# Splits of the last six feed-forward tiles ahead of the down projections: one slot of the border plan in place of two

## The chip, the core and the metric

The kernel runs on one core of a Trainium2 chip. The time is the device time of one execution in microseconds. A core has TensorE (PE, matrix products into PSUM), ScalarE (ACT), VectorE (DVE), GpSimd (POOL) and SyncE (SP, which issues the DMAs here). Each runs its own instructions strictly in the order written, and they meet only at semaphores.

## The reference

One inference step of a two-layer hybrid decoder: 512 prompt tokens and 8 sequences of 8 sample tokens go through the same weights, 576 tokens in all, with a model width of 1024. Each layer has a SwiGLU half-step, a recurrent mixer and a second SwiGLU half-step. Cut to the part that the change touches:

```python
D_MODEL, D_FF = 1024, 2816

def _swiglu(h, w_gate, w_up, w_down):
    return (jax.nn.silu(h @ w_gate) * (h @ w_up)) @ w_down

def _trunk(x, c, states, w):
    for l in range(2):
        f1 = _swiglu(adaln_1(x), w_gate[l, 0], w_up[l, 0], w_down[l, 0])
        x = x + 0.5 * (1.0 + gate1) * f1
        x = x + (1.0 + gate2) * mixer_l(adaln_2(x))
        f2 = _swiglu(adaln_3(x), w_gate[l, 1], w_up[l, 1], w_down[l, 1])
        x = x + 0.5 * (1.0 + gate3) * f2
```

All values are fp32. There are four SwiGLU blocks.

## The kernel before, in words

**Products in three parts.** Every fp32 operand of a matmul is split into a high part (rounded to fp32r) and a low part (the rest). ACT writes the high part (`split_high`, L171), DVE subtracts it from the raw value for the low part (`split_low`, L175), and PE multiplies low by high, high by low and high by high (L1489, L1491, L1493). Weights are split as well as activations. All splits show up in the profile under the two helper lines, so they are told apart by their tiles and widths: a weight piece has 1024, 768 or 512 columns, a hidden tile has 576.

**Stages and pieces.** `dense_chain` builds a chain of stages: `up` (gate and up projections, 22 output tiles of 128), `down` (8 output tiles), projections into and out of the mixers. The program has three such chains with the mixers between them; four `up` stages are each followed by their `down` stage. The work of a stage is cut into pieces, each one weight block in SBUF. The pieces of all stages of a chain are numbered through, and PE goes through them in order, saying `piece_done` after each. In a down stage each output tile has three pieces, with 8, 8 and 6 of the 22 hidden tiles (`DOWN_PIECES`). The hidden tiles come in the order 0 to 6, 8 to 21, 7 (`DOWN_ORDER`).

**Buffers.** Raw weights land in three slots (`RAW`), split weights stand in three places (`SPLIT`). A raw slot is free once its low split is done; then SP issues the next load. A split place is free once PE has ended the piece that stood in it, so the high split of piece i + 3 waits for `piece_done` of piece i.

**Hidden tiles.** Tiles 1 to 7 (`IN_TIME`) are split as they are made. Tile 0 and tiles 8 to 21 (`LATE`) are kept raw in `big_buf` and split later: `hidden_high` (L1609) writes the high part to `low_r` on ACT and says `late_high`, `hidden_low` (L1831) writes the low part to `big_r` on DVE and says `late_low`. At the first output tile of the down stage PE waits before each late tile for its `late_low`.

**The order on ACT and DVE** is one loop over the pieces i in each engine's program, cut here to what runs at a border:

```python
for i in range(total + 1):            # ACT; DVE has low(...) and hidden_low(...) in the same places
    ...
    if i + AHEAD < total:             # AHEAD is 2
        high(i + AHEAD)
    ...
    if i in late_at:
        for kt in late_at[i][1]:
            hidden_high(late_at[i][0], kt)
```

`late_tiles_at` (L1195) is the plan of the late tiles, with `end` for the last piece of the up stage: tile 0 and tiles 8 and 9 in the up stage's last unit, tiles 10 to 12 at `end`, 13 to 15 at `end + 1`, 16 to 18 at `end + 2` and 19 to 21 at `end + 3`. `end + 1` is the first piece of the down stage. So at `end + 2` each engine splits the weights of piece `end + 4` and tiles 16 to 18, and at `end + 3` the weights of piece `end + 5` and tiles 19 to 21. The high splits of tiles 18 to 21 also wait for a piece of the up stage's last unit; in the down stages that have one, the modulation of the next sublayer is computed between the pieces (L123, its weights issued by SP at L116).

Of the kernel before, what the change touches and what calls it, by code (L numbers as in the profile page):

```python
# [1014 lines left out]
def dense_chain(k, stages, begin=False, final=False, early=None, constants=None, stored=None):  # L1015
# [23 lines left out]
    with nc.cleanup_on_exit():  # L1039
# [155 lines left out]
        def late_tiles_at():  # L1195

            plan = {}
            for stage in ups:
                q, end = stage.units[-1].pieces[0][0], stage.last
                for i, tiles in ((q + 1, (0,)), (q + 2, (8, 9)), (end, (10, 11, 12)), (end + 1, (13, 14, 15)),  # L1200
                                 (end + 2, (16, 17, 18)), (end + 3, (19, 20, 21))):
                    plan[i] = (stage, tiles)
            return plan
        late_at = late_tiles_at()
        shift_at, mix_at, high_at, low_at = ({} for _ in range(4))
        for number, stage in enumerate(stages):
# [3117 lines left out]
```

How the kernel before makes its waits and increments, by code:

```python
    def load(self, sp, step):  # L112
        slots = len(self.slot)
        if step >= slots:
            sp.wait_ge(self.done, step - slots + 1)
        sp.dma_start(self.slot[step % slots], self.source[step]).then_inc(self.landed[step % slots], 16)
# [1 line left out]
    def products(self, pe, step):  # L118
        k, slots, width = self.k, len(self.slot), self.per * P
        kt, part, slot = step // self.parts, step % self.parts, step % slots
        pe.wait_ge(self.landed[slot], (step // slots + 1) * 16)
        for j in range(4):
            last = pe.matmul(k.psum[self.banks[part]][32 * j:32 * j + NC_WIDE, 0:width],
                             k.cs[:, kt * NC_WIDE:(kt + 1) * NC_WIDE],
                             self.slot[slot][:, j * width:(j + 1) * width], start=kt == 0, stop=kt == KT - 1)
        last.then_inc(self.done, 1)
# [1 line left out]
    def copy(self, act):  # L128
        act.wait_ge(self.done, self.steps)
        width = self.per * P
        if self.parts == 2:
            act.activation(self.by_vector.rearrange("p (a n) -> p a n", a=2), two_halves(self.k.psum_pair(3), width), ACT.Copy)\
                .then_inc(self.copied, 1)
        else:
            act.activation(self.by_vector, self.k.psum[self.banks[0]][:, 0:width], ACT.Copy).then_inc(self.copied, 1)
# [1 line left out]
    def turn(self, pe):  # L137
        pe.wait_ge(self.copied, 1)
        for part, bank in enumerate(self.banks):
            for b in range(self.per):
                at = (part * self.per + b) * P
```

## Time and profile before

| | us |
|---|---|
| median of three runs | 2674.79 |
| lowest and highest of them | 2669.65, 2676.82 |
| the profiled execution | 2666.39 |
| its span | 2664.7 |

| engine | busy, us | share of the span |
|---|---|---|
| PE, matmuls | 2564.0 | 96% |
| DVE | 1604.7 | 60% |
| ACT | 1056.2 | 40% |
| POOL | 646.3 | 24% |

The granted clock of PE was 0.97 of full speed over the whole execution. To read the profile: the page gives totals and groups of instructions, the waits say which engine stood still for which other one, and the timeline lists one engine's instructions in order of time, with the idle time ahead of an instruction and what ended it in brackets. Matmul records overlap, since they are pipelined: the pace is the distance of their starts, not their length.

### The profile page before, as it was taken

Reading aid. Unit: us, or ns where it says so; the run is one execution under the profiler, and the core shown is the slowest. Engines: PE = TensorE matmul, PEld = TensorE weight load, DVE = VectorE, ACT = ScalarE, POOL = GpSimd, SP = SyncE. Lnnn points to the kernel's source line nnn. Section 1 sums busy time; section 2 is a strip of 40 time slices with the busy share of each in tenths; the row PEclk is TensorE's granted clock in tenths of the full one; section 3 lists DMA queues with packets and bytes.
Section 4 is the critical chain, followed back from the end, with each engine's and each line's share of the span. In section 5 each row is a group of like instructions: output and inputs, shape, how many; then the busy total and the mean of one; then the engine's idle time right before and its main releaser. Section 6 shows DMA issues by size and latency. Waiting matters only on the chain. (4 is left out here: it accounts for less than half of the span.)

```text
span 2664.7 us, 52727 instructions
## 1 busy us (share of the span) xinstructions
PE 2564.0 (96%) x22860; PEld 2410.2 (90%) x22860; DVE 1604.7 (60%) x2302; ACT 1056.2 (40%) x1532; POOL 646.3 (24%) x494
## 2 busy tenths in 40 slices
PE   6999999999999899999999999999999989999998
PEld 4999999887787787999999999999989779999997
DVE  5678626665465555677842677852743256777825
ACT  4444414554344322444432544432432334444513
POOL 0455201000010031255501055500100212355301
PEclk8999999999999979999999999999999789999999
DMA  6332455631100014122255322255751113222324
GB/s 237 105 122 94 154 188 189 244 128 52 34 3 3 9 60 163 64 96 95 94 188 177 120 90 96 96 176 181 233 201 60 50 46 111 71 94 92 99 83 133
DMA packets 80144, 301.60 MB, mean 113 GB/s; under 512 B 8985, under 2 KB 14633, under 8 KB 78633
## 3 DMA queue, kind: packets, MB, share of 16 engines
q1 hardware_dynamic: 79912, 298.23, 33.4%
q8 instruction: 181, 2.97, 0.5%
q14 instruction: 51, 0.41, 0.0%
HBM read 287.45 MB, written 10.74 MB: 112 GB/s over the span
## 5 line engine op out<-in xcount | busy, mean ns | idle before, releaser
L175 DVE TENSOR_TENSOR weights_r<-work,weights_r 128x1024 fp32r<-128x1024 f32 (+2 forms) x309 | 389.6, 1261 | 342.8 <-ACT weights_r L171 342.7
L171 ACT ACTIVATE weights_r<-work 128x1024 fp32r<-128x1024 f32 (+2 forms) x309 | 299.6, 970 | 539.4 <-PE banks L1493 304.0
L1374 POOL TENSOR_TENSOR rows<-rows,consts 128x288 f32<-128x288 f32 (+3 forms) x64 | 82.0, 1282 | 720.0 <-ACT consts L1636 720.0
L1491 PE MATMUL banks<-low_r,weights_r 128*128 128x288 f32 (+1 forms) x1064 | 254.8, 298 | 0.0
L1392 PE MATMUL banks<-big_r,weights_r 128*128 128x288 f32 x768 | 227.0, 296 | 0.0
L1393 PE MATMUL banks<-h_r,weights_r 128*128 128x288 f32 x768 | 226.6, 295 | 0.0
L1391 PE MATMUL banks<-h_r,weights_r 128*128 128x288 f32 x768 | 226.5, 295 | 0.0
L1489 PE MATMUL banks<-h_r,weights_r 128*128 128x288 f32 (+1 forms) x808 | 200.9, 306 | 4.7 <-DVE big_r L437 4.7
L1491 PE MATMUL banks<-big_r,weights_r 128*128 128x288 f32 (+2 forms) x800 | 201.9, 298 | 0.0
L175 DVE TENSOR_TENSOR ring_r<-consts,ring_r 128x1024 fp32r<-128x1024 f32 (+1 forms) x87 | 106.1, 1219 | 155.6 <-ACT ring_r L171 155.6
L1489 PE MATMUL banks<-low_r,weights_r 128*128 128x288 f32 (+2 forms) x720 | 182.5, 303 | 16.9 <-DVE low_r L175 12.0
L1493 PE MATMUL banks<-h_r,weights_r 128*128 128x288 f32 (+1 forms) x808 | 195.0, 299 | 0.0
L1491 PEld LDWEIGHTS banks<-low_r,weights_r 128*128 128x128 f32 x1064 | 181.1, 190 | 0.1
L1493 PE MATMUL banks<-low_r,weights_r 128*128 128x288 f32 (+2 forms) x720 | 179.2, 298 | 0.0
L1391 PE MATMUL banks<-low_r,weights_r 128*128 128x288 f32 x576 | 170.1, 295 | 0.0
L1392 PE MATMUL banks<-low_r,weights_r 128*128 128x288 f32 x576 | 169.9, 295 | 0.0
L1393 PE MATMUL banks<-low_r,weights_r 128*128 128x288 f32 x576 | 169.4, 294 | 0.0
L1489 PEld LDWEIGHTS banks<-h_r,weights_r 128*128 128x128 f32 x808 | 137.5, 190 | 24.2 <-issue 8.9
L171 ACT ACTIVATE ring_r<-consts 128x1024 fp32r<-128x1024 f32 (+1 forms) x87 | 89.8, 1032 | 173.1 <-PE banks L1493 155.4
L1489 PEld LDWEIGHTS banks<-low_r,weights_r 128*128 128x128 f32 x720 | 124.8, 191 | 28.7 <-DVE weights_r L175 13.0
L1393 PEld LDWEIGHTS banks<-h_r,weights_r 128*128 128x128 f32 x768 | 144.8, 189 | 0.0
L1391 PEld LDWEIGHTS banks<-h_r,weights_r 128*128 128x128 f32 x768 | 144.3, 188 | 0.4 <-issue 0.4
(584 smaller groups left out, 7134.4 us busy)
## 6 DMA issues: line engine op xcount, KB each, us to landing
work<-w_ff_dram SPq DMA_DIRECT2D x117, 512.0 KB, 3.4
h<-w_mod_dram SPq DMA_DIRECT2D x48, 768.0 KB, 5.1
consts<-w_ff_dram SPq DMA_DIRECT2D x59, 512.0 KB, 3.4
work<-w_down_dram SPq DMA_DIRECT2D x55, 512.0 KB, 3.6
big_buf<-w_mod_dram SPq DMA_DIRECT2D x24, 768.0 KB, 5.8
consts<-w_down_dram SPq DMA_DIRECT2D x33, 512.0 KB, 3.6
work<-w_down_dram SPq DMA_DIRECT2D x33, 384.0 KB, 3.3
work<-w_mod_first_dram SPq DMA_DIRECT2D x24, 512.0 KB, 12.2
```

The lines of the kernel that those rows point to most:

```text
L171: return act.activation(high, raw, ACT.Copy)
L175: return engine.tensor_tensor(low, raw, high.bitcast(F32), ALU.subtract)
L1374: pool.tensor_tensor(k.rows[:, c], k.rows[:, c], k.square[:, c], ALU.add).then_inc(added, 1)
L1391: pe.matmul(out, low[:, w], x_high, start=j == 0, stop=False)
L1392: pe.matmul(out, high[:, w], x_low, start=False, stop=False)
L1393: last = pe.matmul(out, high[:, w], x_high, start=False, stop=j == KT // 2 - 1)
L1489: pe.matmul(out[a], low[:, w], x[a][0], start=begins, stop=False)
L1491: pe.matmul(out[a], high[:, w], x[a][1], start=False, stop=False)
L1493: last = pe.matmul(out[a], high[:, w], x[a][0], start=False, stop=closes)
```

## The change

Tiles 19, 20 and 21 move from the slot `end + 3` to the slot `end + 2`, behind tiles 16, 17 and 18. The slot `end + 3` has no late tiles any more. The plan is read by ACT and DVE alike, and it holds at all four up stages.

```diff
@@ -1198,7 +1198,7 @@
             for stage in ups:
                 q, end = stage.units[-1].pieces[0][0], stage.last
                 for i, tiles in ((q + 1, (0,)), (q + 2, (8, 9)), (end, (10, 11, 12)), (end + 1, (13, 14, 15)),
-                                 (end + 2, (16, 17, 18)), (end + 3, (19, 20, 21))):
+                                 (end + 2, (16, 17, 18, 19, 20, 21))):
                     plan[i] = (stage, tiles)
             return plan
         late_at = late_tiles_at()
```

In each engine's order the splits of tiles 19 to 21 thereby stand ahead of the split of the weights of piece `end + 5`, where they stood behind it.

## Rows read from the trace of the kernel before

**Rows 1.** The page, part 1: busy time, share of the span, instructions.

```profile
PE 2564.0 (96%) x22860; PEld 2410.2 (90%) x22860; DVE 1604.7 (60%) x2302; ACT 1056.2 (40%) x1532; POOL 646.3 (24%) x494
```

**Rows 2.** PE's waits: who waited for whom, us in total, times, longest us.

```profile
PE banks L1489 <- DVE big_r L175: 6.5, 4, 1.8
```

**Rows 3.** Timeline of PE, first border: start, length, instruction, count, [idle before, releaser].

```profile
311.31 0.43 PE L1489 MATMUL banks<-low_r,weights_r 128*128 128x300 f32 x2
...
312.11 0.43 PE L1489 MATMUL banks<-low_r,weights_r 128*128 128x300 f32 x2
...
314.88 0.54 PE L1489 MATMUL banks<-low_r,weights_r 128*128 128x300 f32 x2 [1.82 <-DVE big_r L175]
...
317.23 0.68 PE L1489 MATMUL banks<-low_r,weights_r 128*128 128x300 f32 x2
...
318.67 0.67 PE L1489 MATMUL banks<-big_r,weights_r 128*128 128x300 f32 x2
...
319.80 0.85 PE L123 MATMUL banks<-h,cs 128*32 128x384 f32 x8
```

**Rows 4.** Timeline of PE, second and fourth border (columns as in rows 3).

```profile
1350.80 0.43 PE L1489 MATMUL banks<-low_r,weights_r 128*128 128x288 f32 x2
...
1354.11 0.53 PE L1489 MATMUL banks<-low_r,weights_r 128*128 128x288 f32 x2 [1.56 <-DVE big_r L175]
...
1356.59 0.43 PE L1489 MATMUL banks<-big_r,weights_r 128*128 128x288 f32 x2
...
1357.48 0.85 PE L123 MATMUL banks<-h,cs 128*32 128x384 f32 x8
...
2521.35 0.43 PE L1489 MATMUL banks<-low_r,weights_r 128*128 128x288 f32 x2
...
2524.66 0.54 PE L1489 MATMUL banks<-low_r,weights_r 128*128 128x288 f32 x2 [1.56 <-DVE big_r L175]
...
2527.95 0.43 PE L1489 MATMUL banks<-low_r,weights_r 128*128 128x288 f32 x2
```

**Rows 5.** Timeline of ACT at the first, third and fourth border.

```profile
307.52 1.82 ACT L171 ACTIVATE low_r<-big_buf 128x576 fp32r<-128x576 f32 x3
311.84 1.06 ACT L171 ACTIVATE weights_r<-work 128x1024 fp32r<-128x1024 f32 x1 [2.50 <-PE banks L1493]
...
1759.89 1.06 ACT L171 ACTIVATE weights_r<-work 128x1024 fp32r<-128x1024 f32 x1 [2.27 <-PE banks L1493]
...
2521.61 1.06 ACT L171 ACTIVATE ring_r<-consts 128x1024 fp32r<-128x1024 f32 x1 [2.20 <-PE banks L1493]
```

**Rows 6.** Timeline of DVE at the first and fourth border.

```profile
308.79 2.09 DVE L175 TENSOR_TENSOR big_r<-big_buf,low_r 128x576 fp32r<-128x576 f32 x3
312.94 1.23 DVE L175 TENSOR_TENSOR weights_r<-work,weights_r 128x1024 fp32r<-128x1024 f32 x1 [2.05 <-ACT weights_r L171]
314.08 2.09 DVE L175 TENSOR_TENSOR big_r<-big_buf,low_r 128x576 fp32r<-128x576 f32 x3
...
2522.71 1.23 DVE L175 TENSOR_TENSOR ring_r<-consts,ring_r 128x1024 fp32r<-128x1024 f32 x1 [1.76 <-ACT ring_r L171]
```

**Rows 7.** Windows: length, busy by engine, then granted clock, DMA share, GB/s.

```profile
316.00:318.00 2.00, 2.00 (x10) 2.00 (x10) 0.17 (x1) 0.00 (x0) 0.00 (x0) 0.50 0.50 199
2525.00:2527.00 2.00, 2.00 (x17) 2.00 (x16) 0.94 (x2) 0.00 (x0) 0.00 (x0) 1.00 0.81 252
```

**Rows 8.** Timeline of SP's queue at the first border.

```profile
303.95 0.43 SPq L116 DMA_DIRECT2D h<-w_mod_dram  x1
...
314.19 0.33 SPq L1274 DMA_DIRECT2D work<-w_down_dram  x1
```

**Rows 9.** The page, part 5 (last column: idle before, releaser) and part 6.

```profile
L171 ACT ACTIVATE weights_r<-work 128x1024 fp32r<-128x1024 f32 (+2 forms) x309 | 299.6, 970 | 539.4 <-PE banks L1493 304.0
...
h<-w_mod_dram SPq DMA_DIRECT2D x48, 768.0 KB, 5.1
```

## The prediction

> **What bounds the kernel now.** I read the page first. TensorE (PE) is busy for 96% of the span [rows 1], so the time is PE's own work plus the gaps in it, and an edit to the order of ScalarE (ACT) and VectorE (DVE) work can only matter where PE waits for one of the two. The table of PE's waits says where: the matmuls of L1489 wait four times for a DVE split (L175) that writes `big_r`, 6.5 us in all, 1.8 us at the longest [rows 2]. The kernel has four borders between an up and a down stage, and the timeline has one such wait at each.
>
> Call the pieces of a down stage D0, D1, D2 (first output tile, 8, 8 and 6 hidden tiles), D3, D4 and so on. In steady work the next hidden tile follows 0.80 us after the last (311.31 and 312.11 in [rows 3]). D2 starts at 311.31, does its first two tiles (17 and 18), and then the third, tile 19, starts at 314.88 and not at 312.91; the row names the DVE split as what it waited for. The same is seen at the third tile of D2 at the other borders, with an idle time of 1.56 us each (at 1354.11, 1762.93 and 2524.66; the second and fourth border stand in [rows 4], the third repeats the pattern).
>
> Why tile 19 is late is seen on ACT and DVE. ACT ends the splits of tiles 16 to 18 at 309.34 and then stands idle for 2.50 us until PE has ended D1, because the next instruction in its order is the split of D4's weights, whose place is that of D1's [rows 5]. Only behind it come the three splits of tiles 19 to 21. DVE is in the same state: idle for 2.05 us, then D4's low part (1.23 us), then the low parts of 19 to 21, the first of which ends at about 314.83 [rows 6]. So a weight split that PE needs more than 8 us later stands ahead of three tile splits that PE needs in 1.6 us.
>
> **The change part by part.** The slot `end + 3` goes and its three tiles join the slot `end + 2`. No instruction is added or taken away, and no DMA and no semaphore: on ACT and on DVE three 576 column splits trade places with the one weight split of D4 (`high(i + AHEAD)` and `low(i + AHEAD)` at `i = end + 3`). Nothing else is issued between the two slots on either engine: the next DVE work on the output tile comes with D2's end.
>
> *What it takes away.* With its third tile in time, D2 would last six tiles of 0.80 us, 4.80 us. It lasts
> - first border: 319.80 - 311.31 = 8.49 us, 3.69 too long [rows 3];
> - second border: 1357.48 - 1350.80 = 6.68, 1.88 too long [rows 4];
> - third border: 6.67 in the same rows of the timeline, 1.87 too long;
> - fourth border: 2527.95 - 2521.35 = 6.60, 1.80 too long [rows 4].
>
> That is 9.24 us. At the first three the handing over to the modulation's matmuls lies in it (1356.59 to 1357.48 is 0.89, 0.09 over a tile [rows 4]), which stays: 9.24 - 0.27 = 9.0 us.
>
> Some 1.8 us of each is the wait itself, the records' 1.56 to 1.82 plus a slow restart. The rest is at the first border alone: there the tiles from 317.23 to 318.67 take 1.44 us and not 0.80, at a granted clock of 0.50, the lower level of 1.2 GHz, where the same stretch of the fourth border has 1.00, 2.4 GHz [rows 7]. Ahead of it PE had worked without a gap and then stood for 1.82 us; its clock fell less than 2 us after. This extra comes to 3.69 - 1.88 = 1.8 us, once in four.
>
> *What it adds.* On ACT the three moved splits take 1.82 us [rows 5], into an idle time of 2.50 us at the first border, 2.27 at the third and 2.20 at the fourth (2.21 at the second): D4's high part is not delayed. On DVE they take 2.09 us into an idle time of 2.05 at the first and 1.76 at the fourth (1.76 and 1.83 at the two between) [rows 6]: D4's low part starts 0.0 to 0.3 us later. Behind it on DVE stands nothing before D2's end, and the load that it frees (that of D7, issued at 314.19 [rows 8]) is needed when PE has ended D4, two pieces of 6.4 us after 316.2 and so 14.8 us later. D4's split ends at about 2524.1 at the fourth border; PE comes to D4 after D2 and D3, at 2526.1 + 6.4 = 2532.5, so 8.4 us are left. I cost the addition at nothing; the cover is PE's work on D2 and D3, and without it the 0.3 us would count four times, 1.2 us.
>
> *What is late next.* Tile 19's low part will end about 0.7 us after those of 16 to 18, near 311.6, and PE asks for it at 312.9; tiles 20 and 21 follow at 0.67 us on DVE and 0.80 on PE. So D2 has no wait left. After D2 come the modulation's matmuls, whose second transfer was issued at 303.95 [rows 8] and which takes 5.1 us in the median [rows 9]: landed by about 309, wanted at 316.2 instead of 319.8. All later loads and splits hang on PE's own progress (a slot is freed by a split, a split by a piece), so they move with it. No wait of PE further on is bound to a clock other than PE's own, and I expect the gain to reach the end.
>
> *The clock, from both sides.* What the wait costs in clock is once 1.8 us and three times nothing in this execution; in another it could be none or all four. Without a fall at any border the sum is 9.0 - 1.8 = 7.2 us; with one at each it is 7.2 + 4 x 1.8 = 14.4 us. I take the traced case, one in four.
> The Trainium skill (TensorE: Matmul & The Clock Gate, Part 1) says that the gate follows how busy the array has lately been, and that the same kernel shows different numbers of slow matmuls from run to run. By that rule the clock falls behind some of these waits and not behind others, as the trace has it, and it may be 7.2 us in one run and more in the next.
>
> **The sum.** 9.0 us of the profiled execution's 2666.39 us (span 2664.7) is 0.34%. The median of the runs shown is 2674.79, 8.4 us above that execution, and the change should take the same absolute time from it: 2674.8 - 9.0 = 2665.8 us. What a measurement of this kernel can tell from no change is about 0.3%, 8.0 us; the three runs before lie 7.2 us apart.
>
> **The rivals.**
> - *No clock to win.* The clock falls at none of the borders in the runs that are timed: 7.2 us, 2667.6. For it: three of four borders. Against: the runs shown are all slower than the profiled one, which speaks for more slow stretches rather than fewer.
> - *More clock to win.* Two to four falls: 10.8 to 14.4 us, 2664.0 to 2660.4. For it: the same 8.4 us of difference.
> - *Given back later.* PE is earlier, and some transfer or a chain on ACT and DVE that was just covered becomes the wait: half is left, 4.5 us, 2670.3. For it: the DMA engines are busy for 0.50 to 0.81 of these stretches [rows 7]. Against: what ACT's weight splits wait for is PE, and the row names no DMA among the larger causes [rows 9].
> - *It doesn't do what it says.* PE waits for something else than the order on ACT and DVE, and the tiles are as late as before: 2674.8. Against: the idle times of both engines stand in the rows, and nothing the three splits need is open by then.
> - *Slower.* The moved splits stand ahead of D4's weights without cover: D4 starts late by 1.82 on ACT and 2.09 on DVE at each border, 15.6 us in all, and the wait for the tiles stays: 2690.4. It decides from the point at which D4's split has no slack; it has 8.4 us, so the three would have to take 8.4 us longer than they do.
>
> **How the numbers follow.** The forecast as summed, one fall or near it, 0.50; no fall 0.22; two and more 0.15; given back 0.08; no effect 0.03; slower 0.02. The run's own scatter of some 3 us lies over all of them. Faster by over 0.3% wants 8.0 us: three quarters of the first, 0.4 of the second (scatter alone), nearly all of the third: 0.37 + 0.09 + 0.14 = 0.60. Slower by over 0.3% is the last case and a trifle of scatter, 0.03. Within 0.3% is the rest, 0.37. For the range: the cases from 2660.4 to 2670.3, of which scatter pushes some beyond; 2659.5 to 2672.0 leaves out the slower case, half of the case without effect and the outermost scatter.
>
> **What would show it.** In the profile of the changed kernel: the row of L1489 waiting for `big_r` four times is gone; six splits of 576 columns stand in one row on ACT and DVE ahead of D4's; D4's high part still starts when PE ends D1; D2 lasts 4.8 us at all four borders, with a granted clock of 1.00. It is wrong if a new wait stands in D3 or D4 or at the modulation's matmuls, if PE's wait at tile 19 is only shorter, or if later stretches at the lower clock become more and eat the gain.

## The result, and the profile after

| | before | after |
|---|---|---|
| median, first comparison (9 runs each) | 2674.21 us | 2658.69 us |
| lowest and highest | 2660.34, 2676.82 | 2646.74, 2665.76 |
| ratio, 95% interval | | 0.9948 (0.9931 to 0.9966) |
| the profiled execution, its span | 2666.39, 2664.7 | 2650.06, 2648.3 |

The medians lie 15.5 us apart; the measured ratio, 0.9948, is 0.52% or 13.9 us of 2674.2. The forecast was 9.0. The profiled execution is 16.3 us shorter. The page of after, parts 1 and 2 (busy time by engine, then the clock granted to PE in 40 equal slices, in tenths), answers to [rows 1]:

```profile
PE 2550.6 (96%) x22860; PEld 2400.3 (91%) x22860; DVE 1602.9 (61%) x2302; ACT 1054.5 (40%) x1532; POOL 646.2 (24%) x494
...
PEclk8999999999989989999999999999999789999999
```

PE's own waits in the table of waits: the row of L1489 waiting for `big_r`, 6.5 us in four times [rows 2], is gone, and what is left between L1489 and a DVE split is the row that stood beside it before, the first tiles of the output projections:

```profile
PE banks L1489 <- DVE low_r L175: 12.0, 2, 6.4
```

The order of the work at the first border, in the timelines of ACT and DVE (start, length, instruction, count, idle time before and what ended it), answers to [rows 5] and [rows 6]:

```profile
307.85 3.54 ACT L171 ACTIVATE low_r<-big_buf 128x576 fp32r<-128x576 f32 x6
311.89 1.06 ACT L171 ACTIVATE weights_r<-work 128x1024 fp32r<-128x1024 f32 x1 [0.51 <-PE banks L1493]
```

```profile
309.12 4.10 DVE L175 TENSOR_TENSOR big_r<-big_buf,low_r 128x576 fp32r<-128x576 f32 x6
313.13 1.22 DVE L175 TENSOR_TENSOR weights_r<-work,weights_r 128x1024 fp32r<-128x1024 f32 x1
```

Six tile splits stand in one row. ACT is still early: 0.51 us of idle time are left ahead of D4's weights, and it is PE that ends them. On DVE the six take 4.10 us and D4's low part follows at once.

The timeline of PE at the first border, in the form of [rows 3]:

```profile
311.63 0.43 PE L1489 MATMUL banks<-low_r,weights_r 128*128 128x300 f32 x2
...
312.43 0.43 PE L1489 MATMUL banks<-low_r,weights_r 128*128 128x300 f32 x2
...
313.23 0.43 PE L1489 MATMUL banks<-low_r,weights_r 128*128 128x300 f32 x2
...
315.63 0.43 PE L1489 MATMUL banks<-big_r,weights_r 128*128 128x300 f32 x2
...
316.52 0.53 PE L123 MATMUL banks<-h,cs 128*32 128x384 f32 x4
```

The third tile, 19, starts at 313.23, 0.80 us after the second. From D2's start to the modulation it is 316.52 - 311.63 = 4.89 us where it was 8.49; and 0.89 of that is still the last tile with its hand-over. PE's granted clock over the same D2, with the modulation's matmuls behind it, in the form of [rows 7]:

```profile
311.63:317.95 6.32, 6.32 (x54) 5.15 (x53) 4.04 (x9) 2.05 (x3) 0.00 (x0) 1.00 0.69 244
```

**Where the time went.** The start of the first down stage and of the three others cut each profiled execution in five. Here are the lengths of the five in us, in all the profiles, with the length of D2 (from its first matmul to the first of D3, all from PE's timeline) at the four borders. At the first three borders the modulation's matmuls lie in that length, 1.4 us. A length with * holds the whole wait that the change takes away. In e3_longer, e4_one_tile and e5_two_tiles the wait is longer or shorter at every border; in e3_longer it stands ahead of D2.

| kernel | start to 1 | 1 to 2 | 2 to 3 | 3 to 4 | 4 to end | D2 at 1, 2, 3, 4 |
|---|---|---|---|---|---|---|
| before | 298.6 | 1039.5* | 408.77* | 761.8* | 156.0* | 9.91, 8.11, 8.10, 6.60 |
| e0_before | 298.5 | 1042.9* | 408.81* | 768.6* | 156.2* | 9.92, 8.11, 8.09, 6.60 |
| e10_before_again | 300.3 | 1037.0* | 408.79* | 765.0* | 155.9* | 8.44, 8.12, 8.10, 6.60 |
| after | 298.9 | 1028.1 | 406.94 | 760.4 | 154.0 | 6.32, 6.30, 6.27, 4.79 |
| e1_after | 300.0 | 1036.9 | 406.98 | 760.2 | 154.1 | 6.32, 6.30, 6.27, 4.78 |
| e7_after_again | 299.3 | 1033.1 | 406.97 | 760.3 | 154.1 | 6.32, 6.30, 6.27, 4.78 |
| e11_after_again | 298.9 | 1038.6 | 406.97 | 767.3 | 154.0 | 6.32, 6.29, 6.28, 4.79 |
| e2_first_only | 298.6 | 1036.3 | 408.80* | 768.7* | 156.2* | 6.31, 8.12, 8.10, 6.60 |
| e6_other_three | 299.6 | 1039.9* | 406.97 | 760.3 | 154.0 | 9.92, 6.30, 6.28, 4.78 |
| e8_third_only | 299.9 | 1043.2* | 408.80* | 758.6 | 156.4* | 9.89, 8.12, 6.28, 6.60 |
| e9_fourth_only | 297.4 | 1027.9* | 408.80* | 762.3* | 154.0 | 8.43, 8.12, 8.09, 4.79 |
| e3_longer | 299.0 | 1043.1 | 413.07 | 767.7 | 158.8 | 7.89, 9.02, 8.99, 6.12 |
| e4_one_tile | 298.1 | 1025.0 | 407.98 | 763.2 | 155.1 | 7.32, 7.31, 7.30, 5.79 |
| e5_two_tiles | 299.0 | 1036.4 | 407.19 | 765.6 | 154.8 | 6.49, 6.51, 6.51, 4.99 |

The even mixer lies between the first and the second border, the odd one between the third and the fourth; the way from the second to the third is dense matmuls alone. There the change gives 408.79 - 406.97 = 1.8 us in every profile, and behind the fourth border 1.9 to 2.4, of which D2 is 1.8. In the first two profiles, before and after, D2 is shorter by 3.59, 1.81, 1.83 and 1.81, 9.04 us, as the sum said. The other 7.3 us of the 16.4 lie, but for some tenths, in one place: the way from the first to the second border is 11.5 us shorter, of which 3.6 is the border and 7.9 is not. The windows of the even mixer show what it is (length, busy by engine, then granted clock), in before, after, e9_fourth_only and e11_after_again:

```profile
956.00:996.00 40.00, 40.00 (x395) 36.22 (x393) 13.23 (x21) 4.87 (x10) 8.34 (x6) 0.62 0.00 1
```

```profile
956.00:996.00 40.00, 40.00 (x440) 34.59 (x441) 19.66 (x31) 6.08 (x13) 12.58 (x9) 0.83 0.19 70
```

```profile
956.00:996.00 40.00, 40.00 (x433) 33.70 (x433) 20.45 (x32) 6.07 (x13) 12.58 (x9) 0.83 0.22 80
```

```profile
956.00:996.00 40.00, 40.00 (x381) 36.31 (x381) 11.90 (x19) 5.46 (x11) 9.02 (x6) 0.57 0.01 1
```

PE is on record as busy throughout and has a granted clock of 0.62 before and 0.83 after; if the stretch goes with the clock, that is 40 x 0.21 = 8.4 us (an estimate). Over the whole way between the two borders, without the border itself, the clock records of the traces have 75.1 us at the lower level before and 58.0 after; half of these 17.1 us is 8.6, beside the 7.9 seen. But a kernel that has all that before has up to that point (e9) shows 0.83 as well, and the changed kernel (e11) shows 0.57. The first two profiles happened to fall on different sides.

### The profile page after: what moved, and what is told of

It is laid out like the page before. It is cut to its first block and busy times, and to the rows that moved or that the text cites. A ratio compares the mean times of both kernels' runs of the same rounds, so it can differ in the third digit from the quotient of the medians.

```text
span 2648.3 us, 52727 instructions
## 1 busy us (share of the span) xinstructions
PE 2550.6 (96%) x22860; PEld 2400.3 (91%) x22860; DVE 1602.9 (61%) x2302; ACT 1054.5 (40%) x1532; POOL 646.2 (24%) x494
## 5 line engine op out<-in xcount | busy, mean ns | idle before, releaser
L1489 PE MATMUL banks<-h_r,weights_r 128*128 128x288 f32 (+1 forms) x808 | 200.5, 306 | 4.7 <-DVE big_r L437 4.7
L1489 PE MATMUL banks<-low_r,weights_r 128*128 128x288 f32 (+2 forms) x720 | 181.6, 301 | 12.0 <-DVE low_r L175 12.0
L1489 PEld LDWEIGHTS banks<-h_r,weights_r 128*128 128x128 f32 x808 | 137.2, 190 | 24.1 <-issue 8.9
L1489 PEld LDWEIGHTS banks<-low_r,weights_r 128*128 128x128 f32 x720 | 124.3, 190 | 23.1 <-DVE weights_r L175 13.0
L1393 PEld LDWEIGHTS banks<-h_r,weights_r 128*128 128x128 f32 x768 | 144.8, 189 | 0.0
L1392 PEld LDWEIGHTS banks<-big_r,weights_r 128*128 128x128 f32 x768 | 144.6, 188 | 0.0
```

The lines of the kernel that those rows point to most:

```text
L1392: pe.matmul(out, high[:, w], x_low, start=False, stop=False)
L1393: last = pe.matmul(out, high[:, w], x_high, start=False, stop=j == KT // 2 - 1)
L1489: pe.matmul(out[a], low[:, w], x[a][0], start=begins, stop=False)
```

## The experiments

The question was whether the 15.5 us are the borders alone with scatter, or whether the change has a gain beyond them. Ratios are to the kernel before on the same chip, with 9 to 12 timed runs of the kernel against 32 to 35 of before; a gain in us is one minus the ratio, times the median of before.

**The kernel before, unchanged.**

> The kernel before, unchanged, for the scatter and for a second profile of it. Question of the study: the change took 15.5 us (ratio 0.9948), where the waits at the four borders and one fall of the clock behind them add up to 9.0. Theory C (clock at the borders): in the runs that are timed PE's clock falls behind more of the four waits than the one that the first profile showed; each fall is worth 1.8 us, so 7.2 + 3 or 4 x 1.8 = 12.6 to 14.4. Theory M (mixers): at most one fall lies at the borders, and the rest comes from stretches at the lower clock far from them, in the mixers, that differ from run to run. Ratio expected by both 1.000, within 0.2%. By C this profile has D2 pieces of 8.4 us at two or more borders; by M at one or none (6.6 to 6.7 at the others), and the time at the lower clock between 960 and 1030 us differs from that of the first profile by several us.

Ratio 1.0014 (0.9996 to 1.0031), the mean of its runs 4.5 us over that of the same program. The clock fell at the first border again (window of e0_before, in its D2) and at no other one, so theory C has no support; D2 as in the table.

```profile
316.00:318.00 2.00, 2.00 (x11) 2.00 (x10) 0.07 (x1) 0.00 (x0) 0.00 (x0) 0.50 0.48 195
```

**The changed kernel, unchanged.**

> The kernel with the change, unchanged, on the same chip as the others. Both theories: no wait at the third tile of D2, D2 4.8 us at all borders. C: the gain comes again at 13 to 15 us, ratio 0.9945 to 0.9951. M: the gain of 15.5 was partly chance; it comes nearer to 9, ratio 0.9960 to 0.9970.

Ratio 0.9973 (0.9953 to 0.9992), just beyond what M gave, at 7.2 us. With nothing altered, half of the first gain was gone, while D2 had its 4.8 us at all borders. This ratio speaks against C, but a later one of the same program, 0.9951 (e7), does not; what rules C out is the table, where none of the profiles with these waits has a fall behind a wait at the second, third or fourth border.

**The first border alone.**

```diff
-                                 (end + 2, (16, 17, 18)), (end + 3, (19, 20, 21))):
+                                 (end + 2, (16, 17, 18) + ((19, 20, 21) if stage is ups[0] and begin else ())),
+                                 (end + 3, () if stage is ups[0] and begin else (19, 20, 21))):
```

> The change at the first border alone, the other three as before. By the waits 1.8 us, with the fall of the clock 3.6 us: ratio 0.9986 to 0.9993. C: D2 of the other three borders lasts 8.4 us in some. M: 6.6 to 6.7 in all or all but one. A third theory, S (shift): to begin the even mixer some us earlier is what shortens the stretch at the lower clock between 960 and 1030 us; then this kernel has that gain as well, 3.6 + 6.5 = 10 us, ratio 0.9962.

Ratio 0.9982 (0.9959 to 1.0005), 3.6 us expected and 4.8 measured by it; the interval holds theory S's 0.9962 too, so it is the profile that answers. D2 is 6.31 at the first border, 8.12, 8.10 and 6.60 at the others. The even mixer was not shortened: 1036.3 us from the first to the second border, which with the 3.6 us of the border is 1039.9, the ordinary length.

**The other three.** The same edit with the condition turned round.

> The change at the second, third and fourth border, not at the first. By the waits alone 3 x 1.8 = 5.4 us, ratio 0.9980. C: each of the three has a share in the falls, up to 10.8 us, ratio 0.9960. M: 5.4 and scatter. S: the even mixer starts when it did, so nothing beyond 5.4.

Ratio 0.9972 (0.9951 to 0.9993), 7.5 us against 5.4; D2 as in the table, with the fall of the clock at the first border. The halves, 4.8 and 7.5, make 12.3 with an error of some 8 us: they say nothing finer than the profiles do.

**Longer waits.** In place of taking the wait away, this makes it longer.

```diff
-                                 (end + 2, (16, 17, 18)), (end + 3, (19, 20, 21))):
+                                 (end + 2, (16,)), (end + 3, (17, 18, 19, 20, 21))):
```

> The opposite of the change: tiles 17 and 18 go behind the split of D4's weights as well (16 at end + 2, 17 to 21 at end + 3). PE then waits at D2's first tile, by the rows of before for 314.83 - 311.31 = 3.5 us at the first border and 3.3 at the others, 1.6 us longer than before. Question: at the first border, where the wait was 2.0 us, the clock fell in all three profiles that had it, at the others, where it was 1.7, in none of eight. Theory L (length): the length of the wait decides, so here the clock falls behind all four, 4 x 1.6 + 3 x 1.8 = 11.8 us slower, ratio 1.0044. Theory P (place): the first border has something of its own (its matmuls of 300 and 276 columns), the other three keep their clock: 6.4 us slower, ratio 1.0024, D2 with its hand-over 9.7 us there and not 11.5.

Ratio 1.0035 (1.0019 to 1.0051), 9.4 us slower. The timeline of PE in e3_longer at the second and fourth border:

```profile
1358.20 0.82 PE L1489 MATMUL banks<-low_r,weights_r 128*128 128x288 f32 x2 [3.22 <-DVE big_r L175]
1359.77 0.68 PE L1489 MATMUL banks<-low_r,weights_r 128*128 128x288 f32 x2
1361.21 0.68 PE L1489 MATMUL banks<-low_r,weights_r 128*128 128x288 f32 x2
...
2538.94 0.82 PE L1489 MATMUL banks<-low_r,weights_r 128*128 128x288 f32 x2 [3.23 <-DVE big_r L175]
```

The window behind the wait at the second border:

```profile
1359.00:1363.00 4.00, 4.00 (x19) 4.00 (x18) 1.73 (x3) 0.00 (x0) 0.00 (x0) 0.50 0.27 108
```

After a wait of 3.2 us tiles follow at about 1.44 us at all four borders, four of them in a row at the second and third, one or two at the first and fourth. The ratio doesn't decide, its interval holds 1.0044 and 1.0024 both; the profile does, and against theory P: a longer wait brings the fall to borders that never had it, and a shorter one (the next run) takes it from the first. Whether place has a share as well, between 1.56 us (only ever seen at the last three borders) and 1.82 us (only at the first), is not shown. The rows of this profile, from the wait on, are longer than those of before by 12.9 us at the four borders (1.4, 4.3, 4.3 and 2.9); the first, where the clock had fallen before as well, has the least of it.

**One tile.** `(end + 2, (16, 17, 18, 19)), (end + 3, (20, 21))`.

> A third of the change: tile 19 alone goes ahead of D4's weights, 20 and 21 stay behind. The wait moves to tile 20 and is one tile's pace shorter, 1.2 us at the first border and 0.9 at the others. L: no fall of the clock at the first border any more, D2 7.4 to 7.6 us with its hand-over, gain 9.05 - 4 x 1.05 = 4.8 us, ratio 0.9982. P: the clock still falls at the first border, gain 3.0 us, ratio 0.9989, D2 9.3 there.

The rows are as L has them: at the first border PE waits 0.74 us for tile 20 and goes on at full clock, and D2 to D3 is 7.32, 7.31, 7.30 and 5.79, which is 5.0 us less than before. PE's timeline of e4_one_tile:

```profile
312.40 0.43 PE L1489 MATMUL banks<-low_r,weights_r 128*128 128x300 f32 x2
...
314.10 0.54 PE L1489 MATMUL banks<-low_r,weights_r 128*128 128x300 f32 x2 [0.74 <-DVE big_r L175]
...
315.00 0.43 PE L1489 MATMUL banks<-low_r,weights_r 128*128 128x300 f32 x2
```

The time is not: ratio 0.9952 (0.9932 to 0.9972), 12.8 us. This is the worst miss of the study, more than the whole change can give at the borders; most of it is the clock, as the last part of this section shows. The profile has the shortest way through the even mixer of all, 1025.0 us.

**Two tiles.** `(end + 2, (16, 17, 18, 19, 20)), (end + 3, (21,))`.

> Two thirds of the change: tiles 19 and 20 go ahead, 21 stays behind. The wait moves to tile 21: 0.4 us at the first border, 0.1 at the others. Gain 9.05 less some 1.0 us, 8 us, ratio 0.9970, by L; by P 1.8 less at the first border if the clock still falls there. D2 with its hand-over 6.4 to 6.8 us.

D2 to D3 is 6.49, 6.51, 6.51 and 4.99, 8.2 us less than before, as expected. Ratio 0.9959 (0.9938 to 0.9981), 11 us, in whose interval the 8 lie.

**The changed kernel again, twice, on two chips.**

> The kernel with the change once more, for the scatter. By the borders, measured in the profiles at 9.05 us (3.60, 1.81, 1.83, 1.81), ratio 0.9966. The first comparison gave 0.9948, the second 0.9973. If the change had a gain of its own beyond the borders, the ratio stays under 0.9955; if that was scatter of the clock in the mixers, it lies at 0.9966 within 0.15%.

Ratio 0.9951 (0.9934 to 0.9968), under the 0.9955 that I had set for a gain beyond the borders, and the interval holds the 0.9966 of the borders too. Not settled by this one.

> The kernel with the change, a fourth time. By the borders 9.05 us, ratio 0.9966; the three comparisons so far gave 0.9948, 0.9973 and 0.9951. R: this one lies within 0.2% of 0.9966, and the mean of the four nears it. S: between 0.9940 and 0.9955. Profile by S: 760.3 us from the third to the fourth border once more.

Ratio 0.9968 (0.9948 to 0.9989), as R has it, and in its profile the way from the third to the fourth border is 767.3 us, not 760.3. That is against theory S.

**The third border alone, the fourth alone.** The first edit with `stage.sublayer == 3`, then with `== 5`, as the condition.

> The change at the third border alone. Question: in ten profiles the way from the first border to the second and from the third to the fourth, which hold the mixers, differs by up to 14 and 7 us beyond what the borders give, while all dense stretches repeat within 0.2 us. From the third to the fourth border, the four profiles with the change there have 760.2 to 760.4 us; the six without have, less what the wait costs there, 760.0 to 766.9. Theory R (scatter): chance, the clock in the mixers falls now here, now there, whatever the borders do. Theory S (shift): to come 1.8 us earlier to the odd mixer is what gives the short way. Time of the border alone 1.8 us, ratio 0.9993 by R; up to 0.9978 by S. Profile: S 760.3 us from the third to the fourth border; R anything from 760 to 767.

Ratio 0.9984 (0.9965 to 1.0004), 4.3 us against 1.8, which the interval holds. The way from the third to the fourth border took 758.6 us, shorter than the 760.3 that S wanted; with e11 the other way, the four equal lengths that had suggested S were chance.

> The change at the fourth border alone, behind both mixers: nothing that it does can reach a mixer. 1.8 us by both theories, ratio 0.9993; profile: from the fourth border to the end 154.1 us where before has 156.1, and before it the times of before, with the scatter in the mixers. If the ratio is off by more than its interval, that is the measure of what a comparison of this kernel can be off by.

Ratio 0.9987 (0.9969 to 1.0005), 3.5 us against 1.8, which the interval holds, and from the fourth border to the end 154.0 us, as expected. This kernel has the wait at the first border, 1.82 us, and there its clock did not fall: D2 to D3 is 8.43.

**The kernel before, once more.**

> The kernel before, unchanged, on another chip, beside the changed one. Ratio 1.000 within 0.2%. Profile: wait and fall of the clock at the first border (8.4 to 8.6 us for D2), wait alone at the other three; by R the ways through the mixers lie anywhere in their scatter.

Ratio 1.0002 (0.9982 to 1.0022). The record has it on chip 5, as e0_before, and not on another one. The first border did not come as expected here either; PE's timeline of e10_before_again, then the window behind the wait:

```profile
316.63 0.53 PE L1489 MATMUL banks<-low_r,weights_r 128*128 128x300 f32 x2 [1.82 <-DVE big_r L175]
...
317.54 0.43 PE L1489 MATMUL banks<-low_r,weights_r 128*128 128x300 f32 x2
...
318.35 0.43 PE L1489 MATMUL banks<-low_r,weights_r 128*128 128x300 f32 x2
```

```profile
317.70:319.70 2.00, 2.00 (x17) 2.00 (x17) 0.21 (x1) 0.00 (x0) 0.00 (x0) 1.00 0.52 209
```

The same wait as in [rows 3] and full clock behind it.

**What all of them say together.** The changed kernel against the kernel before, in four comparisons: the mean of its runs lies 15.4, 7.4, 10.8 and 8.6 us under the other's. All its 42 runs have a mean of 2659.3 us, the 111 of before beside them 2669.1: 9.8 us with a standard error of 1.1, so 7.7 to 11.9. That takes the runs as independent, which they may not be (see e4 and e0). A second way takes the clock out, as an estimate. Every run comes with its mean granted clock; time times clock is about what it would have taken at full clock, if all of it went with the clock. In the three later comparisons this is 2587.9, 2586.2 and 2587.3 us before and 2581.7, 2578.9 and 2579.2 after: 6.2, 7.3 and 8.1, 7.2 us in the mean. The waits alone, from the profile in which no clock fell at the borders, are 8.44 - 6.32 = 2.12, 1.82, 1.83 and 1.81, 7.6 us.

The same reckoning can be made for every kernel of the experiments, beside what its waits alone take from or add to D2 with no fall of the clock. Gains over before, in us, with a standard error of 0.6 to 1.2 for the middle column:

| kernel | at full clock | its waits alone |
|---|---|---|
| e3_longer | -4.9 | -6.4 |
| e0_before, e10_before_again | 1.2, 0.8 | 0 |
| e9_fourth_only, e8_third_only | 0.8, 1.5 | 1.8, 1.8 |
| e2_first_only | 2.8 | 2.1 |
| e4_one_tile | 2.1 | 3.5 |
| e6_other_three | 4.4 | 5.5 |
| e5_two_tiles | 5.3 | 6.8 |
| the change (e1, e7, e11) | 6.2, 7.3, 8.1 | 7.6 |

The gains follow the waits, more taken away giving more, and the two outliers fall in line: e4_one_tile, whose mean is 11.4 us under that of before, keeps 2.1 us of it, and e0_before, 4.5 us over, keeps none. By this estimate the rest of both was clock.

## Why the prediction came out as it did

**What bounds the kernel: right.** PE's waits were the place, and ACT and DVE only through them.

**The waits: right.** 3.69, 1.88, 1.87 and 1.80 less 0.27 of hand-over, 9.0 us; 9.04 in the profiles. The hand-over of 0.89 us stayed. The parts add up in the profiles: the first border alone takes it all there and nothing at the others, and the reverse.

**The clock at the borders: right in kind, its size off.** The clock fell behind the wait of the first border in four of the six profiles that have it, and behind none of the sixteen waits of 1.56 us. I had put 1.8 us to the fall, as the difference between the first border and the others. It is 9.91 - 8.44 = 1.5 us: the wait there is also 0.25 us longer (2.77 us from tile to tile and not 2.52, with or without the fall). The rows have the place where it arises: at the first border ACT begins D4's high part 0.53 us after D2's first matmul (311.84 and 311.31 in [rows 5] and [rows 3]), at the other three 0.26 (2521.61 and 2521.35 at the fourth), in all six profiles with that wait. In the four profiles of the changed kernel, and in e2_first_only, e4_one_tile and e5_two_tiles, the first border has 0.26 too. The mean over runs is then 7.6 + 4/6 x 1.5 = 8.6 us, not 9.0. The no-fall sum was short in the same way, 7.2 us where 7.6 were measured. The rival with more falls never showed: no profile with waits of 1.56 us had one at the other borders, and only waits of 3.2 us brought them there. The rival without a fall is what some of the runs have.

**The addition: right.** Nothing: ACT kept 0.51 us of idle time ahead of D4's weights, where 2.50 - 1.82 = 0.7 follows from the prediction's figures (three more splits took 1.72 us in the row, and PE released ACT 0.27 us sooner after D2's start); DVE's low part of D4 came 0.1 to 0.2 us later in relation to the high part; no wait appeared in D3, D4 or at the modulation.

**Given back later: it was not.** 1.8 us between the second and the third border and 1.9 or more behind the fourth, unspent. On the two ways with the mixers the scatter would hide a loss of a few us; that the runs at full clock keep 7.2 of the 7.6 us leaves little room for one.

**The size: the term that was too small is scatter.** The forecast was 9.0 us and the medians of the first comparison gave 15.5. The forecast time of 2665.8 us stands against a median of 2658.7, or against 2660.9 if the ratio of 0.9948 is taken from the 2674.8 that the forecast began with. The 6.5 us between 9.0 and 15.5 are, by the later comparisons, for the larger part not an effect of the change: 9.8 us with its error stands against 8.6 to 9.0 from the rows. I took the scatter of the runs as 3 us. It is 6 us for a single run (before: 2656.2 to 2678.1 us in 35 runs of one program). The clock makes most of it: the three sets of before scatter by 6.2 to 6.6 us in time and by 1.8 to 2.6 in time times clock. And the mixers are where the clock differs: by the clock records PE is at the lower level for 51 to 89 us on the way from the first to the second border and 55 to 72 from the third to the fourth, and never between the second and the third, e3_longer aside. So a comparison with 9 to 12 runs of a kernel missed the sum of its rows by up to 8 us (e4_one_tile) and a copy of the same program by 4.5 (e0_before). The range, 2659.5 to 2672.0, holds 2660.9 and just misses 2658.7, and it went so low only since it reached for more falls of the clock at the borders, which was not the reason. That the first comparison came out so near its edge and not beyond is luck; the mean of all four, 9.8 us, is what the forecast of 9.0 is to be held against.

**What stays open.** Why the clock stood higher in the runs of e4_one_tile, whose interval leaves out the 0.9981 of its rows, and lower in those of e0_before, whose ratio interval holds 1.000 but whose mean is three standard errors off: it could be something that one loaded program keeps through its runs, or chance. A gain of the change beyond the borders of some 2 us, by way of the mixers' clock, isn't excluded by these numbers; nothing in the profiles shows one. Why ACT comes to D4's weights 0.27 us later at the first border, and only in the kernels with the wait there, wasn't tried. Nor was what parts the four profiles with a fall behind 1.82 us from the two without.

## What to carry to other kernels

In an engine's fixed order, ask of each instruction when its reader wants it, and not in which order the buffers come free: here a weight split that waited for PE itself, and was wanted more than 8 us later, stood ahead of three tile splits wanted within 2 us. Price such a swap from the tile-to-tile distance in PE's timeline, not from the column of idle time, which showed 6.5 us where 9.0 were to be had. And for a gain of a third of a per cent trust the stretches of the profile that repeat to 0.1 us before a ratio of a dozen runs: 408.8 to 407.0 us says more than the whole. Where the runs come with their granted clock, time times clock is a second sieve: here it brought the scatter of a run from 6 us to about 2.

## What the runs showed of the hardware

- **The longer PE's wait, the more often its clock fell.** PE worked densely, waited, and worked on. After 0.74 to 0.77 us (e4_one_tile): none in four. After 1.56 us: none in sixteen. After 1.82 us: four of six, all at the first border. After 3.2 us (e3_longer): four of four. A fall behind 1.82 us cost 1.5 us more, nearly as much as the wait itself. It fell from 1.00 to 0.50 of full speed, 2.4 to 1.2 GHz, 0.9 us after PE had gone on in the first profile, and at the last three borders of e3_longer while PE still waited. The Trainium skill (TensorE: Matmul & The Clock Gate, Part 1) lets the clock depend on recent activity and the count of slow matmuls differ from run to run; the trace agrees, at 8.44 and 9.92 us for the same D2 of the same program.
- **PE can be on record as busy without a gap and have little more than half its clock.** In the 40 us of the even mixer shown above all 40.00 are busy, at a granted clock of 0.57, 0.62 or 0.83. By an estimate this stretch alone moves a run by up to 10 us (40 x 0.26); the whole way from the first to the second border was 1025.0 to 1043.2 us long.
- **Dense stretches repeat far better than the whole.** 406.94, 406.98, 406.97 and 406.97 us in four executions whose spans are 2648.3, 2658.1, 2653.7 and 2665.7.
